# Filling steps and convolution taps gathered in the first and third level of a triangular inverse, in a two-layer hybrid encoder

## What is computed

```python
    def step(state, inp):
        r_t, w_t, k_t, v_t, a_t, b_t = inp
        sa = jnp.einsum("bhij,bhj->bhi", state, a_t)
        state = (state * w_t[:, :, None, :] + sa[..., None] * b_t[:, :, None, :]
                 + v_t[..., None] * k_t[:, :, None, :])
        return state, jnp.einsum("bhij,bhj->bhi", state, r_t)
...
    y_fwd = rwkv7_scan(rh, heads(decay[:, :, 0]), heads(k_dir[:, :, 0]), vh, -kk,
                       kk * heads(iclr[:, :, 0]), reverse=False)
    y_bwd = rwkv7_scan(rh, heads(decay[:, :, 1]), heads(k_dir[:, :, 1]), vh, -kk,
                       kk * heads(iclr[:, :, 1]), reverse=True)
```

## Time and profile before

| | us |
|---|---|
| median of 3 runs | 2916.6 |
| lowest and highest | 2916.3, 2918.51 |
| the profiled execution | 2916.94 |
| its span, first to last instruction | 2915.2 |
| TensorE busy | 2717.1 (93%) |
| VectorE busy | 1461.1 (50%) |
| ScalarE busy | 458.0 (16%) |

### The profile page before, as it was taken

The page is one execution under the profiler, slowest core; times in us unless marked ns, Lnnn a source line. Parts: engine busy times, 40 slices in busy tenths (PEclk is TensorE's granted clock), DMA queues, the critical chain, the costliest instruction groups (busy, mean ns, idle before and its releaser), DMA issues.

```text
span 2915.2 us, 53917 instructions
## 1 busy us (share of the span) xinstructions
PE 2717.1 (93%) x23805; PEld 1921.3 (66%) x23805; DVE 1461.1 (50%) x2622; ACT 458.0 (16%) x936; POOL 239.2 (8%) x372
## 2 busy tenths in 40 slices
PE   4999999999998989899989999999999988898998
PEld 3766777777774445377766668777777744445775
DVE  4452346776766756313035423666766677562001
ACT  0000122221212213100010011322212122121000
POOL 7000101000001101010000010110000010000000
PEclk9999999999999999999999999999999999998999
DMA  9794333222226443374559733332222353433442
GB/s 335 278 333 160 121 113 116 84 85 94 93 86 226 138 141 111 120 287 136 167 212 333 257 123 138 133 113 85 80 91 89 135 185 130 137 110 130 144 150 96
DMA packets 226057, 444.31 MB, mean 152 GB/s; under 512 B 7432, under 2 KB 102214, under 8 KB 225824
## 3 DMA queue, kind: packets, MB, share of 16 engines
q1 hardware_dynamic: 211136, 395.59, 38.8%
q0 software_dynamic: 12960, 38.98, 4.2%
q10 hardware_dynamic: 1728, 6.29, 0.5%
HBM read 422.88 MB, written 17.96 MB: 151 GB/s over the span
## 4 chain that ended last, share of the span: by engine, by line
PE 77%; DVE 10%; DMA 7%; issue 2%; ACT 2%; POOL 1%; SPq 1%; DVEq 0%; ACTq 0%; POOLq 0%
PE ps L973 75%; DVE scratch L1949 3%; DMA ring<-in_ffn_w 3%; DVE scratch L1952 2%; DMA scratch<-fill_scratch 2%; DMA scratch<-in_ada_w 1%; DVE merged L2171 1%; DVE scratch L1955 1%; DVE scratch L2185 1%; DMA scratch<-acs_scratch 1%; DMA ring<-in_w_in 1%; DVE x L1955 0%; PE ps L1006 0%; ACT scratch L1916 0%; POOL scratch L940 0%
## 5 line engine op out<-in xcount | busy, mean ns | idle before, releaser
L973 PE MATMUL ps<-hT,ring 128*128 128x256 f32 (+1 forms) x4992 | 1151.6, 385 | 14.9 <-DVE hT L1952 10.7
L973 PEld LDWEIGHTS ps<-hT,ring 128*128 128x128 f32 (+1 forms) x4992 | 930.2, 190 | 178.8 <-issue 34.2
L973 PE MATMUL ps<-scratch 64*64 64x32 f32 (+7 forms) x15136 | 860.7, 255 | 73.3 <-ACT scratch L1889 26.9
L973 PEld LDWEIGHTS ps<-scratch 64*64 64x64 f32 (+4 forms) x15136 | 569.9, 140 | 396.7 <-issue 230.1
L1949 DVE TENSOR_TENSOR scratch<-scratch,ps 128x256 f32<-128x256 f32 (+3 forms) x304 | 153.6, 505 | 749.6 <-ACT scratch L1651 649.6
L973 PE MATMUL ps<-ring,hT 128*128 128x256 f32 (+1 forms) x1280 | 428.3, 482 | 6.4 <-DVE hT L2613 4.9
L973 PEld LDWEIGHTS ps<-ring,hT 128*128 128x128 f32 x1280 | 238.3, 193 | 155.0 <-issue 126.6
L1949 DVE TENSOR_TENSOR scratch<-scratch 128x512 f32<-128x512 f32 (+5 forms) x450 | 296.7, 659 | 71.5 <-DMA scratch<-acs_scratch 24.9
L973 PE MATMUL ps<-ring,scratch 128*128 128x512 f32 x512 | 237.4, 602 | 1.5 <-DVE scratch L1952 1.0
L1651 ACT ACTIVATE scratch<-ps 128x512 f32<-128x512 f32 x44 | 26.3, 597 | 900.0 <-PE ps L973 900.0
L1955 DVE SCALAR_TENSOR_TENSOR scratch<-scratch,ccol 128x1024 f32<-128x1024 f32 x126 | 162.7, 1291 | 4.6
(11 more groups left out here) (216 smaller groups left out, 1412.8 us busy)
## 6 DMA issues: line engine op xcount, KB each, us to landing
ring<-in_w_in SPq DMA_DIRECT2D x56, 2048.0 KB, 8.9
ring<-in_ffn_w SPq DMA_DIRECT2D x88, 1024.0 KB, 10.0
scratch<-in_ada_w SPq DMA_DIRECT2D x36, 2048.0 KB, 14.2
scratch<-in_ffn_w SPq DMA_DIRECT2D x44, 1024.0 KB, 5.0
scratch<-acs_scratch POOLq DMA_DIRECT2D x32, 512.0 KB, 5.0
ring<-in_w_branch_mamba SPq DMA_DIRECT2D x8, 2048.0 KB, 7.9
scratch<-fill_scratch SPq DMA_DIRECT2D x4, 2048.0 KB, 14.2
ring<-in_w_branch_rwkv SPq DMA_DIRECT2D x4, 2048.0 KB, 12.0
```

The costliest lines, as they stand in the source:

```text
L973: return pe.matmul(o, lhsT, rhs, start=start, stop=stop)
```

## The change

The table of filling steps and the condition of the convolution taps are changed. In each pair levels 0 and 2 get four filling steps and levels 1 and 3 none; in the six pairs with a convolution levels 0 and 2 get four taps and levels 1 and 3 none. The counts of a pair stay the same (8 and 8), and so does the order among the steps and among the taps.

```diff
-FILL_PAIR = (("ops", 12), ("mid", 8), ("lv", 8), ("k0", 2), ("k1", 2), ("k2", 2), ("k3", 2),
+FILL_PAIR = (("ops", 12), ("mid", 8), ("lv", 8), ("k0", 4), ("k1", 0), ("k2", 4), ("k3", 0),
...
-                        if k < LV - 1 and p in CONV_AT_LEVELS:
-                            convolve(2)
+                        if k in (0, 2) and p in CONV_AT_LEVELS:
+                            convolve(4)
```

## The result

| | median us | runs | ratio to the kernel before |
|---|---|---|---|
| before | 2917.25 | 4 (2916.3 to 2918.51) | |
| changed | 2938.94 | 4 (2933.71 to 2941.04) | 1.0049, 95% interval 1.0029 to 1.0068 |

The changed kernel is slower; 2912.4 had been forecast, and the time lies far above the range. The two medians alone give 1.0074; all four runs of the changed kernel are in the fast state, and why the ratio on record is smaller isn't known. The profiled execution has a span of 2939.0 us, 23.8 more than the one before.

A forecast was written before the change was run, and what follows sets the result against it. TensorE, busy for 93% of the span, was taken to bound the kernel. Two levels get 0.132 us shorter, 32 times, 4.2 us less, giving 2912.4 us against the median 2916.6; range 2907.0 to 2918.5 us.

The forecast's parts named there:

- The levels: Levels inside a head pair: 4.26 us with four filling steps, 2.40 us with none, against 3.395 us before.
- the 0.20 us a group: TensorE's filling groups: 0.20 us is paid once for a group whatever its size, and 32 groups vanish.
- the 0.066 us of wait that comes back: In 32 unfilled levels, a wait of 0.066 us that two filling steps did hide shows again.
- the 4.2 us in all: Over all pairs of levels: 32 x 0.132 us less, 4.2 us gained.
- rival 3: Unfilled levels: the correction products run in sequence where no filling stands ahead, 9.9 us slower, 2926.5 us; chance 0.03.
- rival 4: Filling groups: only the group price counts, the hidden wait does not come back; 6.3 us less, 2910.3 us; chance 0.11.
- The taps at nothing: VectorE's convolution taps in filled levels: four hide behind the filling steps, leaving 0.17 us idle, so they cost nothing.
- The price if the cover is gone: VectorE's taps: once the 0.17 us idle time is used up, every 0.1 us beyond it costs 2.4 us.
- The loads into the ring start earlier by as much: Weight loads into the ring: filling units end at most one level earlier and loads start earlier by as much.
- Rival 1: Unfilled levels: code comes late beside weight loads, five more standstills and two more clock falls, +7.4, 2924.0 us; chance 0.06.
- The argument that the filled level slows the draw as much as the unfilled one speeds it up: Against rival 1: four filling steps slow the level before by as much, so the mean instruction draw is equal.
- Rival 5: Standstills and clock falls in the levels are dealt anew and half goes: -9.2, 2907.4 us; chance 0.14.

The follow-up runs named there:

- spread: The kernel before with eight weight loads of a layer, one in each pair, started with the first level: 2951.83 us, ratio 1.01.
- gathered: The changed kernel with eight weight loads of a layer, one in each pair, started with the first level: 2954.66 us, ratio 1.0091.

## Why the prediction was wrong

- **The levels** (4.26 and 2.40 us, the 0.20 us a group, the 0.066 us of wait that comes back, the 4.2 us in all) were right to the hundredth of a microsecond, and with the loads out of the way the sum was 4.0 us in the median. Rivals 3 and 4 are refuted by the same rows: 1.15 us from mask to gain (rival 3), and 6.66 us for two levels, where rival 4 wants 6.59.
- **The taps at nothing** was right, with 0.17 us left as worked out. The price if the cover is gone, 2.4 us for each 0.1, was too small: taps in the unfilled levels came 0.68 us late there, which gives some 16 us by it, and cost 44, since the clock went with them.
- **"The loads into the ring start earlier by as much"** is the step that failed. It was noted and costed at nothing. In pair 2 it put a 2 MB load beside the two unfilled levels at the end; moving that one load back was worth 13.5 us. On that chip the changed kernel loses 17.2 us against the kernel before and misses 4.2 of gain, 21.4 in all; the 7.9 left are, by elimination, what the sum had left out beside the other loads: longer standstills and the clock that falls behind them.
- **Rival 1** named the mechanism and had a chance of 0.06. Its prices were too small. It had five more standstills of 1.12 us, 5.6 in all; in the levels there were four more, but the nine were longer (1.86 us in the mean against 1.12), which is 11.1 more in all. It had two more clock falls of 3.0 us; there were six more, with 37.4 us at half clock. A standstill of over 1 us in the levels lowered the clock in three of four cases in the kernel before and its variant with small loads, in ten of ten in the changed kernel and its variant; in the pairs with all loads beside the levels it was four of seven spread and seven of nine gathered. The argument that the filled level slows the draw as much as the unfilled one speeds it up doesn't fit the lengths: with the same loads beside the levels the gathered kernel's standstills are 1.94 us in the mean, the spread one's 1.19. That a late block is met at one place and not in the mean is my reading of it; no run isolates it.
- **Rival 5**, that the standstills are dealt anew and some go, had 0.14 and the wrong sign (it also took 5 us for half of 11.6, which is 5.8). There was no deal: each standstill of the two kernels stands beside or right behind a load, and all but the one of 0.80 us beside a weight load.
- The Trainium skill, Runtime: NRT & Kernel Launch, Instruction fetch mechanics, says that crossing a 16 KiB block is mostly hidden. By count that is so: the kernel before has 187 instruction packets and six such standstills in the pairs. Beside a bulk load it is not: in these traces each of the 15 standstills of the two kernels ends 2.2 to 2.6 us after the start of an instruction packet of 16,384 bytes, and up to 3.13 us are lost. By the page rival 1 would have cost nothing.

What stays open: what in the DMA engines delays the packet (its own transfer took 0.9 to 1.2 us; why it started late isn't in the trace); that TensorE waits for just that packet is inferred from the constant 2.2 to 2.6 us; and how long a fall lasts (3.4 to 17.1 us were seen).

## What to carry to other kernels

Before moving work of the busiest engine, list what its completion triggers on the queues, and where a transfer that starts earlier will run: a saving of 4 us inside a loop can move a 2 MB load onto a stretch of dense small instructions and lose 13 us. Where a trace shows idle time with no semaphore beside a saturated DMA, try the load elsewhere first; here one added wait for each of five loads of a layer was worth 15 us to the kernel before, nearly four times what the change itself could bring. And a wait that leaves TensorE short of work is to be priced with the clock that goes with it.

## What was unexpected of the hardware

- TensorE stands still beside bulk loads, and each standstill of the two kernels ends 2.2 to 2.6 us after the start of an instruction packet: 5.6 us in the levels before, 16.7 changed, none once the loads were elsewhere, with the same 444 MB moved.
- A delay of one microsecond can cost several: behind most standstills of over 1 us the granted clock fell to 0.5, for 3.4 to 17.1 us, half of which is lost at most.
- The clock also falls with no standstill and no load beside the levels: 15 falls in 12 pairs came with 0.68 us of additional waiting in levels of 2.40 us.
- Two sets of 64x64 products on different quarters of the array take nearly the time of one also when no filling stands ahead of them: 1.15 us from mask to gain with both sets, 1.12 with one.
